# A two-block transformer on one core: SBUF addresses aligned to 2048 bytes, the first stages reordered, two norms taken together

## The chip, the cores and the metric

The kernel runs on one core of a Trainium2 chip, as one program launched once. The metric is its device time in microseconds (us). 302 weight tiles of 512 KB are streamed from HBM while the program runs.

## What is computed

512 tokens, width 1024, float32. A first block of two layers, then a second block of one layer:

```python
for i in range(2):                       # first block
    hn = rmsnorm(x, attn_norm_g[i])
    mix, q_cross = mla_mixer(...) if i == 0 else swa_mixer(...)   # 12 heads; full causal, or window 128 with alibi and sinks
    cross = memory_cross_attention(q_cross, rmsnorm(mem), w_mem_kv[i])   # 4 heads, 256 memory tokens
    x = x + concat(mix, cross) @ w_o[i]
    x = x + relu(rmsnorm(x, g) @ w_up) ** 2 @ w_down              # 4096 hidden
x = rmsnorm(x, final_norm_g)
h = rmsnorm(x, norm1_g)                  # second block: the norm of a norm
...                                      # gated convolution, compressed and windowed attention (8 heads), merge
x = x + mix @ w_o
x = x + (silu(conv(h2 @ w_g)) * (h2 @ w_u)) @ w_ffn_out           # 2816 hidden
```

In the first layer the queries come from a rank-384 and keys and values from a rank-256 projection, each with its own norm (`c_q`, `c_kv`); 32 of the 96 query and key features are rotated by position, and the rotated key part is the same for all heads.

## The kernel before

**Data.** Activations lie feature-major: 128 features on the partitions, 512 tokens along the row, `X[:, k, :]` for the k-th 128 features. Every matrix product is made of three in a reduced float32 format: an operand is split in a high part (rounded) and a low part (the rest), and `product` issues high x high, high x low, low x high (L526, L527, L528). `XH`/`XL` hold the split activation (8 slices), `HH`/`HL` the hidden layer of the two MLPs, `H2H`/`H2L` that of the last, `MIXH`/`MIXL` and `YAH`/`YAL`/`YBH`/`YBL` the merge of the second block.

**Weights.** A ring of four slots. SyncE loads tile n into `RAW` once the low part of tile n-4 is made; ScalarE copies it to `WH` (high part, L835); GpSimd (POOL) computes `WL = RAW - WH` in four pieces (L487). ScalarE calls `keep_ahead(o)` between its other operations: it makes high parts up to three tiles ahead of the tile that output o ends with, and waits there until the old tile of the slot has been used.

**Products.** `dense` walks through a stage's outputs in order. An output is 8 steps over k of three products each, 512 columns wide, into one of four PSUM banks; output o waits until output o-4 has been drained by VectorE (`drained`). Between outputs a stage can have steps in `after`: `sums(norm)` adds squares over the partitions, `scales(norm)` spreads the norm's factor over them, `rotate_query(h)` turns one head's query. The order of each engine's queue is written out by hand; engines wait for one another by counting semaphores alone.

**Norms.** The norm's factor per token is not applied to the operand but to the result. For each slice ScalarE squares into `SQ` (L870), VectorE adds into `ACC` (L1175, L1178), and the square waits for the add before. Then `sums`, VectorE's variance (L1192), ScalarE's root, VectorE's diagonal of factors (L1201), `scales`, and a copy to `RBC` (L1209). `x_hi` (L877) and `x_lo` (L1214) write XH and XL from X times the gain.

**Start.** `in0` (8 outputs: two for c_kv, three for c_q, the rotated key, two for the memory queries), `mem` (8 outputs of 256 columns: memory keys and values for both layers), `up0` (26 outputs: six of keys, four and four of values, twelve query heads), then the first attention. VectorE drains nearly all of it; its queue in order: `c_kv` scaling, `c_q` squares, memory drains (`mem_out`, L1241, L1432), splits of the memory queries (L1248) and of layer 0's memory keys (L1257), the angles for the rotation (16 operations, L1266 to L1275), key rotation, splits of layer 1's memory keys, key drains (L1227), value drains (L1472, L1475), the query operand (L1418, L1423), then head by head the query rotation (L1480 to L1490). ScalarE copies the rotated key rows to each of the 12 heads (L1029).

**Output projections** (`output_projection`, stages wo0, wo1). The next MLP reads XH/XL too, which hold the projection's operand. ScalarE waits until the last output's last product and then rewrites slices 0 to 3, VectorE follows, and then 4 to 7.

**Second attention** (64 units of up to 256 keys, four steps in a row over VectorE, ScalarE and TensorE each). Ahead of it VectorE drains eight outputs and splits each (L1243, L1248, L1249), six for the 12 heads (Q1), two for the memory queries (`QX`, used from unit 48 on), and then zeroes one column in three banks (L1535); TensorE waits for all of it.

**Between the blocks.** mlp1's last outputs are followed by the squares of `final`. `in2` (25 outputs) runs on; behind outputs 0 and 1 come sums and scales of `final`, behind 2 and 3 those of `norm1`, whose squares are made in between, serially. Then VectorE multiplies and sums the position embeddings of the compression (L1555, L1556), copies `RBC`, drains outputs 0 to 3 to R32 (L1583), multiplies X by the final norm (L1715), and makes the angles of the second block.

## Time and profile before

| | |
|---|---|
| device time, median of three runs | 2014.95 us (2013.19 to 2016.40) |
| device time of the profiled execution | 2013.64 us |
| its span, first to last instruction | 2011.7 us |
| TensorE busy | 97% |
| mean granted TensorE clock | 0.987 of full speed |
| VectorE, ScalarE, GpSimd busy | 44%, 38%, 46% |

A row of the timeline gives start and length in us, engine, line, operation, what is written from what, and in brackets how long the engine was idle before and what ended it. PE is TensorE's matmul, DVE VectorE, ACT ScalarE, POOL GpSimd. Buffer numbers are left out of names, so R is R32 or any like it. Matmuls overlap in such rows; the distance between starts is what one costs.

### The profile page before, as it was taken

The numbers are of one execution on the slowest core, as the hardware profiler recorded it, in microseconds if no ns is written. First come the engines' busy times: TensorE is split into PE (matmuls) and PEld (weight loads), VectorE is DVE, ScalarE is ACT, GpSimd is POOL, SyncE is SP. The second block draws the span as 40 slices with busy tenths as digits, with TensorE's granted clock in tenths as the row PEclk, the third lists the DMA queues.
The fourth block names the chain that finished last, engine by engine and source line by source line (L and its number), as shares of the span: only waits on it lengthen the run. The fifth ranks groups of instructions, "written<-read, shape, count | busy, mean of one in ns | idle before, by whom it ended". The sixth has DMA issues, their size and how long they took to land.

```text
span 2011.7 us, 27171 instructions
## 1 busy us (share of the span) xinstructions
PE 1946.1 (97%) x9314; PEld 1588.4 (79%) x9314; DVE 887.5 (44%) x1848; ACT 771.3 (38%) x1379; POOL 931.5 (46%) x1236
## 2 busy tenths in 40 slices
PE   7889999999999989999999998999999999999999
PEld 5756878888888878788888875678988888888887
DVE  5787733222225576322222268686722245444200
ACT  4446833232223467432232333335832233222221
POOL 5541045555555651555555554342045546655553
PEclk9989999999999999999999998999999999999999
DMA  5220022322222310222323232121022223223332
GB/s 212 95 74 22 1 84 85 101 97 94 94 94 84 102 51 18 89 95 94 98 94 101 91 115 73 42 74 43 2 73 95 94 84 105 94 94 100 98 104 74
DMA packets 46686, 167.67 MB, mean 83 GB/s; under 512 B 5312, under 2 KB 5632, under 8 KB 46336
## 3 DMA queue, kind: packets, MB, share of 16 engines
q1 hardware_dynamic: 45216, 162.55, 24.7%
q10 hardware_dynamic: 1376, 3.84, 0.5%
q8 instruction: 62, 1.02, 0.2%
q14 instruction: 32, 0.26, 0.0%
HBM read 164.28 MB, written 2.10 MB: 83 GB/s over the span
## 4 chain that ended last, share of the span: by engine, by line
PE 57%; DVE 4%; issue 2%; ACT 1%; DVEq 0%; ACTq 0%
PE bank L526 17%; PE bank L528 17%; PE bank L527 17%; PE bank L626 2%; PE bank L599 1%; PE bank L612 1%; ACT PROB L896 1%; PE bank L768 1%; DVE ACC L1178 0%; PE bank L623 0%; PE bank L730 0%; ACT XH L902 0%; DVE KNL L1257 0%; ACT SQ L870 0%; PE bank L722 0%
## 5 line engine op out<-in xcount | busy, mean ns | idle before, releaser
L487 POOL TENSOR_TENSOR WL<-RAW,WH 128x256 fp32r<-128x256 f32 x1208 | 913.8, 787 | 1036.0 <-ACT WH L835 1035.9
L526 PE MATMUL bank<-XH,WH 128*128 128x512 f32 (+1 forms) x1480 | 592.3, 400 | 42.1 <-POOL WL L487 13.7
L527 PE MATMUL bank<-XL,WH 128*128 128x512 f32 (+1 forms) x1480 | 581.3, 393 | 0.0
L528 PE MATMUL bank<-XH,WL 128*128 128x512 f32 (+1 forms) x1480 | 581.0, 393 | 0.0
L835 ACT ACTIVATE WH<-RAW 128x1024 fp32r<-128x1024 f32 x302 | 317.0, 1051 | 348.0 <-PE bank L528 345.5
L526 PEld LDWEIGHTS bank<-XH,WH 128*128 128x128 f32 (+1 forms) x1480 | 279.6, 189 | 117.1 <-issue 28.0
L527 PEld LDWEIGHTS bank<-XL,WH 128*128 128x128 f32 (+1 forms) x1480 | 279.5, 189 | 62.5 <-issue 4.1
L528 PEld LDWEIGHTS bank<-XH,WL 128*128 128x128 f32 (+1 forms) x1480 | 279.3, 189 | 61.5
L528 PE MATMUL bank<-HH,WL 128*128 128x512 f32 x512 | 202.2, 395 | 0.0
L526 PE MATMUL bank<-HH,WH 128*128 128x512 f32 x512 | 202.2, 395 | 0.0
L527 PE MATMUL bank<-HL,WH 128*128 128x512 f32 x512 | 202.2, 395 | 0.0
L1339 DVE TENSOR_TENSOR AB<-TMP 128x512 f32<-128x512 f32 x64 | 44.3, 692 | 264.1 <-ACT TMP L933 264.1
L1356 DVE TENSOR_TENSOR DT<-bank,RB 128x512 f32<-128x512 f32 x64 | 44.3, 692 | 230.7 <-PE bank L528 230.7
L933 ACT ACTIVATE TMP<-bank 128x512 f32<-128x512 f32 x64 | 38.3, 599 | 222.9 <-PE bank L528 222.8
L527 PEld LDWEIGHTS bank<-HL,WH 128*128 128x128 f32 x512 | 96.1, 188 | 23.4
L528 PEld LDWEIGHTS bank<-HH,WL 128*128 128x128 f32 x512 | 96.1, 188 | 23.3
L526 PEld LDWEIGHTS bank<-HH,WH 128*128 128x128 f32 x512 | 96.1, 188 | 23.3
L870 ACT ACTIVATE SQ<-X 128x512 f32<-128x512 f32 x48 | 30.3, 631 | 148.8 <-DVE ACC L1178 107.4
L526 PE MATMUL bank<-H2H,WH 128*128 128x512 f32 x176 | 69.8, 396 | 0.0
L527 PE MATMUL bank<-H2L,WH 128*128 128x512 f32 x176 | 69.8, 396 | 0.0
L528 PE MATMUL bank<-H2H,WL 128*128 128x512 f32 x176 | 69.8, 396 | 0.0
L1152 ACT ACTIVATE TMP<-TMP,GV 128x512 f32<-128x512 f32 x22 | 16.0, 726 | 121.5 <-DVE TMP L1609 121.5
(334 smaller groups left out, 2577.5 us busy)
## 6 DMA issues: line engine op xcount, KB each, us to landing
RAW<-stream SPq DMA_DIRECT2D x302, 512.0 KB, 3.6
X<-x SPq DMA_DIRECT2D x4, 512.0 KB, 7.5
out<-X SPq DMA_DIRECT2D x8, 256.0 KB, 4.4
MEM<-mem ACTq DMA_DIRECT2D x1, 1024.0 KB, 10.9
W<-cmp_w ACTq DMA_DIRECT2D x1, 1024.0 KB, 6.1
CT<-consts ACTq DMA_DIRECT2D x1, 656.0 KB, 13.2
POSB<-pos_rows ACTq DMA_DIRECT2D x2, 256.0 KB, 5.1
HR<-pos_rows ACTq DMA_DIRECT2D x1, 256.0 KB, 2.7
```

What stands on the lines that cost most here:

```text
L487: ins = pool.tensor_tensor(WL[:, slot, c], RAW[:, slot, c], WH[:, slot, c].bitcast(F32), ALU.subtract)
L526: pe.matmul(dst, lhs[0], rhs[0], start=start, stop=False)
L527: pe.matmul(dst, lhs[0], rhs[1], start=False, stop=False)
L528: return pe.matmul(dst, lhs[1], rhs[0], start=False, stop=stop)
L599: ins = pe.matmul(BANK[SCORES[i % ns]][:, u.keys], q, k, start=n_pass == 0, stop=n_pass == len(u.passes) - 1)
L612: ins = pe.transpose(BANK[TURNED[j % nt]][:, blk(kb)], row[:, blk(kb)], IDENT)
L626: ins = pe.matmul(BANK[HEAD_OUT[u.head % 2]][:, u.out_cols], u.values[kb], pt[j % len(pt)][:, blk(kb)], start=u.start and kb == 0, stop=u. ...
L835: act.activation(WH[:, slot, :], RAW[:, slot, :], ACT.Copy).then_inc(hi_done, 1)
L870: act.activation(SQ[:, 0:tokens], src, ACT.Square, scale=scale).then_inc(squared, 1)
L933: act.activation(TMP[:, m % 2, :], BANK[(o0 + m) % RING][:], ACT.Relu).then_inc(signal(name + "_relu"), 1)
L1339: dve.tensor_tensor(AB[:, m % 2, :], TMP[:, m % 2, :], TMP[:, m % 2, :], ALU.mult).then_inc(drained, 1)
L1356: dve.tensor_tensor(DT[:, m % 2, :], BANK[(o0 + 8 + m) % RING][:], RB2[:], ALU.mult).then_inc(drained, 1)
```

## The change

- **Addresses.** Every SBUF tensor whose row is a multiple of 2048 bytes starts at a multiple of 2048; the others at one of 32, as all did. CT, GV and GF are declared behind ACC, SQ, TMP, RBC and COS/SIN, some tensors move, and one is added (`KMV`).
- **Start.** MEM, the positions and the late constants are loaded through SyncE's queue behind the first weight tiles instead of ScalarE's. The first output is computed in three passes over k (all high x high, then high x low, then low x high). The squares of in0 and mem alternate between two buffers. The angles are made in two parts: one ahead of the drain of output 3, one ahead of the c_kv adds; ScalarE's two sines follow the c_q root and stand ahead of the query splits. `rotate_key`, `sums("c_q")` and `scales("c_q")` move to other outputs. ScalarE drains the values; one DMA places the key rows in the 12 heads. The splits of layer 0's memory keys go behind the query operand, those of layer 1 behind the first attention.
- **Output projections.** Each k-step of the last output signals that its slice of XH/XL has been read; ScalarE and VectorE rewrite slices 0 to 6 as these come, and slice 7 once X is final. `x_hi` and `x_lo` come before the square and the add, there and in the MLPs.
- **Second attention.** The two memory queries are drained to buffers of their own (`QX1`) and split inside the attention, ScalarE's part at units 3 and 6, VectorE's at 6 and 9; TensorE waits for them at unit 48.
- **Norms.** norm1's squares are made with those of final behind mlp1's last outputs, in separate buffers; both sums follow output 0 of in2, both scales output 1. The embeddings of the compression move behind output 3, the second block's angles ahead of mlp1's last chunk, the multiplication of X by the final norm into the merge.

```diff
-            return stack.enter_context(nc.sbuf_tensor(name, shape, dt))
+
+            row = 4 * math.prod(shape[1:])
+            return stack.enter_context(nc.sbuf_tensor(name, shape, dt, align_bytes=32 if row % 2048 else 2048))
...
+        QX1 = [KMV[:].rearrange("p a n -> p (a n)"), POSF1]
...
-            for j in range(1, RING):
-                load(j, j, stream[j])
+            load(1, 1, stream[1])
+            load(2, 2, stream[2])
+            sp.dma_start(MEM[:], mem).then_inc(mem_in, 16)
+            load(3, 3, stream[3])
+            sp.dma_start(POSB0[:], pos_rows[0]).then_inc(signal("pos_in"), 16)
+            sp.dma_start(POSI[:], pos_cols).then_inc(signal("pos_in"), 16)
+            sp.dma_start(CT[:, CONST_LATE:], consts[:, CONST_LATE:]).then_inc(signal("late_consts_in"), 16)
...
+            def first_output(steps):
+
+                pe.wait_ge(hi_done, 1)
+                for n_pass, (w, a) in enumerate(((WH, XH), (WH, XL), (WL, XH))):
+                    if n_pass == 2:
+                        pe.wait_ge(lo_done, 1)
+                    for t, c, width, k, o, _, _, _ in steps:
+                        if n_pass < 2:
+                            pe.wait_ge(signal("in0_x_hi" if n_pass == 0 else "in0_x_lo"), k + 1)
+                        ins = pe.matmul(BANK[o % RING][:], w[:, t % RING, c:c + width], a[:, k, :],
+                                        start=n_pass == 0 and k == 0, stop=n_pass == 2 and k == KD - 1)
+                ins.then_inc(products_done, 1)
+
             pe.wait_ge(consts_in, 32)
-            dense(lambda _: plan.steps["in0"], 0, operand(XH, XL),
...
-                  after={0: [scales("c_kv")], 2: [sums("c_q")], 4: [scales("c_q")], 6: [rotate_key]})
+                  after={0: [scales("c_kv")], 1: [rotate_key], 3: [sums("c_q")], 6: [scales("c_q")]})
...
                     if m == KD - 1 and not own_operand:
-                        act.wait_ge(products_done, plan.out_mark[o0 + KD - 1])
-                        for j in range(KD // 2):
+                        for j in range(KD - 1):
+                            act.wait_ge(signal(stage + "_operand_read"), j + 1)
                             x_hi(x_stage, norm, j)
                     act.wait_ge(drained, o0 + m + 1)
+                    if own_operand or m == KD - 1:
+                        x_hi(x_stage, norm, m)
                     square(norm, m, X[:, m, :])
-                    if own_operand:
-                        x_hi(x_stage, norm, m)
-                if not own_operand:
-                    for m in range(KD // 2, KD):
-                        x_hi(x_stage, norm, m)
...
+                            x_hi(stage_after, gain_after, m)
                             square(norm_after, m, X[:, m, :])
-                            if stage_after:
...
-            for h in range(NH):
-                act.activation(KT0[HD:QK, h, :], KR[HD:QK, :], ACT.Copy).then_inc(signal("key_placed"), 1)
-                keep_ahead(up0 + 3 + h // 2)
-                if h == 3:
+            act.dma_start(KT0[HD:QK, :, :], KR[HD:QK, :].unsqueeze(1).to_broadcast([ROPE, NH, S])
+                          ).then_inc(signal("key_placed"), 16)
+            for o in range(6, 14):
+                keep_ahead(up0 + o)
+                if o == 10:
                     c_hi(KKV, KQ)
-            for o in range(9, 14):
-                keep_ahead(up0 + o)
...
+            dve.wait_ge(signal("pos_in"), 32)
+            angles0(0)
...
+            angles0(1)
             add_square("c_kv", 0)
             add_square("c_kv", 1)
...
             mem_out(1)
             mem_out(2)
+            mem_out(3)
             scale_columns("c_q", P * KQ, factor=-MLA_SCALE)
-            mem_out(3)
             for j in range(2):
                 split_lo_q(j, PROB1[:, j, :], QX[:, 2 * j:2 * j + 2, :])
-            for j in range(2):
-                split_lo_k(2 + j, PROB1[:, 2 + j, 0:NMEM], KMH[:, 0, 2 * j:2 * j + 2, :], KML[:, 0, 2 * j:2 * j + 2, :])
-            dve.wait_ge(signal("pos_in"), 32)
-            angles(POSB0[:], POSF0[:], const("inv_mla"), ANG0[:, 0, :], ANG0[:, 1, :], COS0[:], SIN0[:], "angles0")
             for o in range(4, 6):
...
-                split_lo_k(4 + j, PROB1[:, j, 0:NMEM], KMH[:, 1, 2 * j:2 * j + 2, :], KML[:, 1, 2 * j:2 * j + 2, :])
+            mem_out(6)
+            scale_rows("c_q", ACC)
+            mem_out(7)
             up0 = plan.out0["up0"]
             for m in range(6):
                 both_halves(up0 + m, KT0[0:HD, :, :], m)
-            for b in range(NT):
-                dve.tensor_copy(V0[:, b, S:NH * HD], output(up0 + 6 + b)[:, 0:NH * HD - S]).then_inc(drained, 1)
             c_scale("c_q", KKV)
-            for b in range(NT):
-                dve.tensor_copy(V0[:, b, 0:S], output(up0 + 10 + b)[:]).then_inc(drained, 1)
-            dve.wait_ge(signal("key_placed"), NH)
+            for j in range(2):
+                split_lo_k(2 + j, PROB1[:, 2, j * NMEM:(j + 1) * NMEM], KMH[:, 0, 2 * j:2 * j + 2, :],
+                           KML[:, 0, 2 * j:2 * j + 2, :])
+            dve.wait_ge(signal("key_placed"), 16)
+            dve.wait_ge(drained, up0 + 14)
             for h in range(NH + 1):
...
             attention("mla")
+            for j in range(2):
+                split_lo_k(4 + j, KMV[:, j, :], KMH[:, 1, 2 * j:2 * j + 2, :], KML[:, 1, 2 * j:2 * j + 2, :])
             output_projection("wo0", "mlp0", "mlp0")
...
-                    split_value(in1 + 6 + m, s1 + 2 + m, PROB1[:, (2 + m) % 4, :], RBC, -SCALE)
-                if m >= 1:
-                    dst = Q1[:, 2 * m - 2:2 * m, :] if m <= 6 else QX[:, 2 * m - 14:2 * m - 12, :]
-                    split_lo_q(s1 + 1 + m, PROB1[:, (1 + m) % 4, :], dst)
+            for m in range(8):
+                split_value(in1 + 6 + m, s1 + 2 + m, PROB1[:, (2 + m) % 4, :] if m < 6 else QX1[m - 6], RBC, -SCALE)
+                if 1 <= m < 7:
+                    split_lo_q(s1 + 1 + m, PROB1[:, (1 + m) % 4, :], Q1[:, 2 * m - 2:2 * m, :])
             dve.wait_ge(drained, in1 + 14)
             for b in SCORES:
                 dve.memset(BANK[b][:, 2 * P:2 * P + 1], 0.0).then_inc(signal("column_zeroed"), 1)
...
+            def memory_queries(j):
+                return lambda: split_lo_q(s1 + 8 + j, QX1[j], QX[:, 2 * j:2 * j + 2, :])
+
+            attention("swa", {6: memory_queries(0), 9: memory_queries(1)})
...
             scale_columns("final", D, diagonal=TMP[:, 0, :])
-            for m in range(KD):
-                add_square("norm1", m)
-            scale_rows("final", TMP[:, 1, :])
-            scale_columns("norm1", D, of_normed=True)
-            dve.wait_ge(signal("w_cmp_in"), 32)
-            for x_, name in enumerate(("pe_k", "pe_v")):
...
-            own.step(dve.memset(VC[:], 0.0))
-            own.step(dve.memset(KCH[:].bitcast(F32), 0.0))
-            own.step(dve.memset(KCL[:].bitcast(F32), 0.0))
-            own.step(dve.tensor_scalar(gain("q"), gain("q"), -SCALE, None, ALU.mult))
+            scale_columns("norm1", D, of_normed=True, bank=7)
+            scale_rows("final", FINAL)
+            scale_rows("norm1", RBC, bank=6)
+
...
                 if what == "out" and j == 3:
-                    for m in range(KD):
-                        dve.scalar_tensor_tensor(X[:, m, :], X[:, m, :], gain("final", m), TMP[:, 1, :],
-                                                 ALU.mult, ALU.mult).then_inc(signal("x_normed"), 1)
-                    dve.wait_ge(signal("pos2_in"), 16)
-                    angles(POSB2, POSF2, const("inv_nsa"), PROB2[:, 0, :], PROB2[:, 1, :], COS2[:], SIN2[:],
-                           "angles2")
+                    prepare_compression()
...
+                dve.scalar_tensor_tensor(X[:, m, :], X[:, m, :], gain("final", m), FINAL[:], ALU.mult, ALU.mult
+                                         ).then_inc(signal("x_normed"), 1)
+            dve.wait_ge(signal("x_normed"), KD)
```

## Rows read from the trace of the kernel before

**Rows 1.** The page's busy times

```profile
PE 1946.1 (97%) x9314; PEld 1588.4 (79%) x9314; DVE 887.5 (44%) x1848; ACT 771.3 (38%) x1379; POOL 931.5 (46%) x1236
```

**Rows 2.** Waits of TensorE over the whole span: us, times, longest

```profile
PE bank L526 <- POOL WL L487: 13.7, 2, 13.3
PE bank L526 <- DVE PROB L1241: 8.6, 1, 8.6
PE bank L526 <- DVE R L1583: 8.3, 1, 8.3
PE bank L526 <- DVE KT L1227: 5.9, 2, 5.6
PE bank L599 <- DVE bank L1535: 4.6, 1, 4.6
PE bank L526 <- issue: 4.2, 2, 2.1
```

**Rows 3.** Windows over dense stages: length, PE busy (products), granted clock, DMA

```profile
389.53:433.06 43.53, 43.53 (x193) 1.00 0.30 96
433.06:477.86 44.80, 44.80 (x194) 1.00 0.29 95
1598.55:1643.53 44.98, 44.98 (x193) 1.00 0.28 94
1884.71:2008.40 123.69, 123.69 (x529) 1.00 0.28 92
```

**Rows 4.** Windows behind long gaps, TensorE alone

```profile
93.80:130.10 36.30, 21.44 (x85) 0.76 0.20 71
298.00:301.40 3.40, 3.40 (x9) 0.51 0.24 98
```

**Rows 5.** Timelines of ScalarE, GpSimd and TensorE at the start: start, us, what

```profile
13.54 1.33 ACT L877 ACTIVATE XH<-X,GV 128x512 fp32r<-128x512 f32 x2 [1.59 <-DMA X<-x]
...
16.69 1.04 ACT L835 ACTIVATE WH<-RAW 128x1024 fp32r<-128x1024 f32 x1
...
17.81 7.41 POOL L487 TENSOR_TENSOR WL<-RAW,WH 128x256 fp32r<-128x256 f32 x8 [4.67 <-ACT WH L835]
...
21.58 0.50 PE L526 MATMUL bank<-XH,WH 128*128 128x512 f32 x1 [0.38 <-POOL WL L487]
```

**Rows 6.** Timeline of VectorE ahead of the first attention

```profile
47.44 0.42 DVE L1209 COPY ACC<-bank 128x256 f32<-128x256 f32 x1 [3.31 <-PE bank L580]
...
86.59 6.55 DVE L1257 TENSOR_TENSOR KML<-PROB,KMH 64x256 fp32r<-64x256 f32 x8
93.17 0.43 DVE L1266 CAST POSF<-POSB 128x512 f32<-128x512 int32 x1
...
101.62 0.43 DVE L1275 TENSOR_SCALAR SIN<-SIN 128x512 f32<-128x512 f32 x1
...
108.20 6.84 DVE L1257 TENSOR_TENSOR KML<-PROB,KMH 64x256 fp32r<-64x256 f32 x8
...
123.70 1.47 DVE L1472 COPY V<-bank 128x256 f32<-128x256 f32 x4
...
128.05 1.47 DVE L1423 TENSOR_TENSOR XL<-TMP,XH 128x512 fp32r<-128x512 f32 x2
```

**Rows 7.** Second attention: VectorE's timeline; window (PE, PEld, DVE, ACT, POOL)

```profile
724.02 1.43 DVE L1248 TENSOR_TENSOR QX<-PROB,QX 64x512 fp32r<-64x512 f32 x1
...
732.00:745.00 13.00, 12.49 (x104) 11.67 (x105) 12.90 (x65) 11.95 (x46) 4.99 (x8) 1.00 0.00 1
```

**Rows 8.** Timeline of VectorE between the two norms and R32

```profile
1212.36 0.69 DVE L1178 TENSOR_TENSOR ACC<-ACC,SQ 128x512 f32<-128x512 f32 x1 [0.79 <-ACT SQ L870]
...
1219.65 1.76 DVE L1555 TENSOR_TENSOR PROB<-W,GV 128x1024 f32<-128x1024 f32 x1
```

**Rows 9.** Two products in a row in a down stage, TensorE's timeline

```profile
450.32 0.40 PE L528 MATMUL bank<-HH,WL 128*128 128x512 f32 x1
450.56 0.39 PE L526 MATMUL bank<-HH,WH 128*128 128x512 f32 x1
```

More of the change, by code:

```diff
@@ L17 @@
+import math
 from contextlib import ExitStack
@@ L179, with square_no, squares_end @@
 NORM_K = dict(NORMS)
+def square_no(norm, m):
+    if norm in ("final", "norm1"):
+        return SQUARES0["final"] + 2 * m + (norm == "norm1")
+    return SQUARES0[norm] + m
+def squares_end(norm):
+    return SQUARES0["norm1"] + KD if norm == "final" else SQUARES0[norm] + NORM_K[norm]
 def over(fn, i, n=NCH):
@@ L452, in program, with squares_of, squares_sum @@
             IN2 += AFTER_OUT.get(o, [])
+        def squares_of(norm, m):
+            if norm == "norm1":
+                return TMP[:, 0, :]
+            return TMP[:, 1, :] if norm in ("in0", "mem") and m % 2 else SQ
+        def squares_sum(norm):
+            return TMP[:, 1, :] if norm == "norm1" else ACC
         block = ctx.enter_context(nc.Block())
@@ L528, in product, with dense @@
                 return pe.matmul(dst, lhs[1], rhs[0], start=False, stop=stop)
-            def dense(steps_of, i, act, n_tok=S, token_major=(), ready=None, after=None, seen=None):
+            def dense(steps_of, i, act, n_tok=S, token_major=(), ready=None, after=None, seen=None, o0=None, released=None):
                 seen = set() if seen is None else seen
@@ L577, in step @@
                     if n:
-                        pe.wait_ge(scale_used, n)
+                        pe.wait_ge(scale_used, n - (norm == "norm1"))
                     pe.wait_ge(diag_done, n + 1)
-                    pe.matmul(BANK[5][:, 0:tokens], ONES, diagonal[:, 0:tokens], start=True, stop=True
+                    pe.matmul(BANK[bank][:, 0:tokens], ONES, diagonal[:, 0:tokens], start=True, stop=True
                               ).then_inc(scale_done, 1)
@@ L689, in _ @@
             rotate_query(NH - 1)()
-            attention("mla", (drained, plan.out0["wo0"]), (signal("split_lo"), SPLIT_AT["in1"]))
-            dense(lambda _: plan.steps["wo0"], 0, operand(XH, XL), ready=heads_ready("mla"))
+            attention("mla", (drained, plan.out0["wo0"]), (signal("split_lo"), SPLIT_AT["mem"] + 2))
+            dense(lambda _: plan.steps["wo0"], 0, operand(XH, XL), ready=heads_ready("mla"),
+                  released=signal("wo0_operand_read"))
             mlp("mlp0")
@@ L698, in _ @@
             attention("swa", (drained, plan.out0["wo1"]), (signal("column_zeroed"), len(SCORES)),
-                      (signal("split_lo"), SPLIT_AT["in2"]))
-            dense(lambda _: plan.steps["wo1"], 0, operand(XH, XL), ready=heads_ready("swa"))
+                      (signal("split_lo"), SPLIT_AT["in2"] - 2))
+            dense(lambda _: plan.steps["wo1"], 0, operand(XH, XL), ready=heads_ready("swa"),
+                  released=signal("wo1_operand_read"))
             mlp("mlp1")
@@ L748, in compress @@
                               start=True, stop=True).then_inc(signal("cmp_sums"), 1)
-            after = {0: [sums("final")], 1: [scales("final", diagonal=TMP[:, 0, :])],
-                     2: [sums("norm1")], 3: [scales("norm1")]}
+            after = {0: [sums("final"), sums("norm1", bank=7)],
+                     1: [scales("final", diagonal=TMP[:, 0, :]), scales("norm1", bank=6)]}
             def turn_gates(_):
@@ L1051, in _ @@
             std("in1")
-            for o in range(15):
-                if o < 14:
-                    keep_ahead(in1 + o)
+            for o in range(14):
+                keep_ahead(in1 + o)
                 if 1 <= o < 3:
@@ L1072, in _ @@
             std("final")
-            for m in range(KD):
-                square("norm1", m, X[:, m, :], scale=gain("final", m))
-            keep_ahead(in2 + 2)
             std("norm1")
@@ L1186, in scale_columns @@
                 if of_normed:
-                    own.then(dve.tensor_scalar(VAR[:, 0:nt], BANK[4][:, 0:nt], 1.0 / width, None, ALU.mult))
+                    own.then(dve.tensor_scalar(VAR[:, 0:nt], BANK[bank][:, 0:nt], 1.0 / width, None, ALU.mult))
                     for _ in range(2):
@@ L1261, in split_lo_k, with angles @@
                 ins.then_inc(signal("split_lo"), 1)
[L1263 removed]
+            def angles(pos, posf, inv, angle, turns, cos, sin, done, parts=(0, 1)):
                 c1 = TWO_PI_PARTS
[L1266 to L1268 removed]
+                if 0 in parts:
+                    own.then(dve.tensor_copy(posf, pos))
+                    own.then(dve.tensor_scalar(angle, posf, inv, None, ALU.mult))
+                for dst, quarter in [((cos, 0.25), (sin, 0.0))[part] for part in parts]:
                     own.then(dve.tensor_scalar(turns, angle, 1.0 / (2 * np.pi), quarter, ALU.mult, ALU.add))
@@ L1312, in output_projection @@
                 for m in range(KD + 1):
+                    if m == KD - 1 and not own_operand:
+                        for j in range(KD - 1):
+                            x_lo(x_stage, norm, j)
                     if m < KD:
```

205 lines of the change are left out of this document (108 added, 97 removed).

## Prediction

> **What bounds the kernel now.** I read the page's busy times first: TensorE is busy 1946.1 of 2011.7 us [rows 1], so a microsecond counts only if it shortens TensorE's own sequence. That sequence can shorten in three ways: idle time goes, a product takes less time, or less work runs at the halved clock. The waits of TensorE give the first [rows 2]: some 48 us, of which 13.7 is mostly the start, 8.6 a wait for a VectorE copy in the memory projection, 8.3 a wait for R32, 5.9 for the key copies, 4.6 for the zeroed column ahead of the second attention, 4.2 twice 2.1 behind an output projection. The windows over whole dense stages give the second [rows 3]. A stage is 192 products of 512 columns (528 in the last), plus at most two that overlap an edge. An "up" stage, operand XH/XL, takes 43.53/192 = 0.2267 us a product. The "down" stage beside it, operand HH/HL, takes 44.80/192 = 0.2333, the stage on MIXH/MIXL 44.98/192 = 0.2343, the last, on H2H/H2L, 123.69/528 = 0.2343. All are 100% busy at full clock, so this is no wait. The third: after a long gap the clock is at its lower level for a while (0.51 over 3.4 us behind the output projection, 0.76 on average in 93.8 to 130.1, which holds two gaps and half-clock stretches) [rows 4].
>
> **Alignment.** What separates the fast operand from the slow ones? Not the work beside it: the last stage has almost none and is slow. From the declared sizes (rounded to 32 bytes), XH, XL, WH and WL all sit at one offset modulo 2048 bytes. HH sits 1408 further on (CT 6368 + GV 896 + GF 32 + SM 224 + POSI 32 = 7552), H2H at 1440, MIXH at 928. The change puts all of them at a multiple of 2048, so each has the relation to WH that XH has today. I charge them XH's rate: HH/HL 1536 products x 6.6 ns = 10.2; H2 528 x 7.6 = 4.0; MIX 192 x 7.6 = 1.4; YA and YB 192 x about 6.6 = 1.3 (not shown apart; by HH's rate). Sum **16.9 us**. The bounds are 0 (the offset is not the cause) and 16.9 + 29.3 (XH's 4440 products would gain another 6.6 ns each).
> A rule speaks against this term: the Trainium skill, page "SBUF — State Buffer", section "SBUF: two separate sides", says contention is structural and that PE's ports wait on nobody. All these offsets are multiples of its 16-byte line, so by it the term is 0. The trace disagrees in that equal products differ by 6.6 ns, but it cannot show that the address is why. That is the second rival.
>
> **From the start to the first attention.** Today TensorE waits for the low half of tile 0, since each of output 0's products by k needs it, and starts its second output at 21.58, when POOL has finished tile 1: high half at 16.69, POOL from 17.81 [rows 5]. Ahead of that high half ScalarE lost 1.59 us waiting for the last of x, with which 1 MB of MEM shared the DMA engines, and some more for an add. With both gone the high half is at about 14.3, POOL's 3.7 us end at 19.1, and TensorE, which has meanwhile done output 0 pass by pass, goes on about 2.3 earlier; two short waits behind it (the sum of squares, C32) go too. Head start at output 4, an estimate: 3.2.
> Then VectorE's queue decides [rows 6]. The angles are 16 operations, 93.17 to 102.05, 8.9 us. Their first part (4.9) moves ahead of c_out(3), where VectorE idles 3.31 today. The second (4.0) stands ahead of the c_kv squares, and TensorE's sums("c_kv") waits for those. My step-by-step times: the adds end near 63.5, TensorE arrives at 60.4, **a new wait of 3.1**; and the c_kv diagonal comes 1 us later than today, for three drains now follow the adds. The head start is gone; TensorE begins memory output 4 about 1.2 later than today.
> Behind it the gain comes. VectorE is busy without a break from 82.84 to 129.5, and its XL for the queries ends this queue [rows 6]. Out of it go the key splits of layer 0 (6.55) and layer 1 (6.84), the angles (8.9) and V copies (1.47): 23.7. Against that: 1.2 late, 2.7 waiting for ScalarE (its sines now stand ahead of the query split: 1.3 table load, two of 0.6), about 1.5 for ScalarE's V copies between the c_hi steps. XL is ready near 110. TensorE itself needs, from 93.0: six outputs of 1.36, four of 0.72, four of 1.36, 16.5 us, and arrives at 109.8. Output 14 starts at 109.8 instead of 130.2; 1.2 us of waiting for ScalarE's TMP goes as well: 21.7. The key splits of layer 0 (6.6) now stand ahead of the query rotation and make VectorE 4 us late there; it catches up 0.8 a head, and bank and rotation are needed four heads later: nothing. The key rows become one DMA of 0.8 MB, nearly 20 us ahead of its use: nothing. POOL takes about 3.7 us a tile [rows 5] and each tile of this stretch arrives 1 to 3 us early: nothing, with little cover. A gap of 3 us or the thin outputs at 100 to 104 may lower the clock once more (3.4 us at half, 1.7). I take **20**, with 12 and 23 as bounds.
>
> **Output projections.** XH's slices are now rewritten as the last output releases each, so ScalarE's 0.7 and VectorE's 0.8 run under its 5.45 us. The slice of k = 7 comes 2.4 to 4 us after its last product and is needed 4.8 after. Both 2.1 us waits (2.25 between products) go [rows 2], and at the first the stretch at clock 0.51 (3.4 us, so 1.7) [rows 4]: 4.0 + 2.2. The order "XL before the add" takes about 0.7 from the wait at the second layer's start. **6.9**. The moved key splits of layer 1 (6.8 VectorE, 3.4 ScalarE) lie under the first four outputs of wo0, 21.8 us.
>
> **Second attention.** Four QX operations, 3.6 us, come out from between the last value and the zeroed columns [rows 7]. They return at units 6 and 9, with 2.5 us on ScalarE. There VectorE is busy 12.90 of 13 us and ScalarE 11.95 [rows 7]: nearly no cover. I take **1** (bounds -1 and 4).
>
> **Two norms together.** Today norm1's eight squares and eight adds alternate until 1213.05; the diagonal follows until 1219.7; two operations of 1.8 us for each of two position embeddings, 7.3 us, then stand ahead of RBC, and TensorE waits 8.3 us for R32, until 1229.25 [rows 8, 2]. After the change the squares lie under mlp1's last outputs: VectorE's share there is 0.7 + 0.9 + three of 0.7 to 1.2, about 5.2 of 5.45, just covered. TensorE waits 0.3 for the last add, takes both sums behind output 0 and both diagonals behind output 1 (a wait of 0 to 1.5), and runs outputs 2 and 3; RBC is there by 1210, so output 4 starts at 1219.9 at the latest 1221: 9.4. The half clock behind the old gap goes; by the stretch of [rows 4] I put 1.9. The embeddings now delay only R32[4], whose bank is needed 21 us later. The angles (9 to 12 us) move ahead of mlp1's last chunk, where four free banks (22.7 us) cover them. The rescaling of X (8 x 0.75) moves into merge, 16.5 us a step with 5 of VectorE. **11.5** (8 to 13). The 2 us waits in the rest of in2 come from work that stays.
>
> **Sum.** 16.9 + 20 + 6.9 + 1 + 11.5 = 56.3; the profiled execution took 2013.64, so 1957.3. The median of the runs shown is 1.3 higher: **1958 us**.
>
> **Rivals.**
> 1. *Queues give less*: the c_kv wait grows, the clock falls again, the attention takes all back. Bounds: 12 + 5 - 1 + 8 = 24 instead of 39.4: 1974. For it: VectorE's full queue; against it: TensorE's idle rows are large and plain.
> 2. *The address does nothing*: 1958 + 16.9 = 1975. For it: the trace changes address and tensor together (by the rule of the skill this is the outcome); against it: four operands, one rate per offset, whatever runs beside them.
> 3. *Both*: 1991.
> 4. *XH gains as well*, because its own offset was not a multiple of 2048: 1958 - 29 = 1929. Nothing in the trace shows a faster product at full clock.
> 5. *Slower*: multiples of 2048 are a bad offset for all products. Single products of the slow operands take 0.24 [rows 9]. If all 6888 did: 4440 x 13.3 + 2448 x 6.4 ns = 75 us, against 39.4 saved: 2049. It decides once the mean rises over today's 229.2 ns by 39.4/6888 = 5.7, beyond every stage mean shown. Against it: XH and WH share an offset today.
>
> **How the numbers follow.** Forecast (1946 to 1968) 0.58, rival 1 0.15, rival 2 0.12, rival 3 0.05, rival 4 0.07, rival 5 0.03. The range 1940 to 1980 holds the forecast and rivals 1 and 2. Faster by over 0.2% (what a measurement here tells from no change) needs 4 us: all but rival 5 and a little for what I have not seen: 0.94; same 0.02, slower 0.04.
>
> **What would show it.** HH, H2H and MIXH stages at 0.2267 a product; no wait at R32 or behind wo0/wo1; a new wait of about 3 us for the c_kv adds; first attention from 147 instead of 167; the second attention longer by 2 to 3 us. Wrong if those stages keep 0.233, or the XH stages change.

## The result, and the profile after

The changed kernel takes **1970.4 us** (median of 4 runs, 1969.3 to 1970.7) against 2015.7 (2013.2 to 2017.5) before: ratio 0.9775, 95% interval 0.9758 to 0.9792. Forecast was 1958, with 1940 to 1980 as range. 56.3 us were forecast, 43.2 are gone from the span (2011.7 to 1968.5).

Two measures are used below. Rows of waits give TensorE's idle time alone. A "gap" in the text is the time from the start of one product to the start of the next, so it is 0.3 to 0.6 us longer than the idle time in it.

The page's busy times (answers to [rows 1]), and the waits of TensorE ([rows 2]; the first row is the time until the first product):

```profile
PE 1932.1 (98%) x9314; PEld 1590.0 (81%) x9314; DVE 897.3 (46%) x1840; ACT 770.5 (39%) x1375; POOL 944.3 (48%) x1236
```

```profile
PE bank L703 <- ACT WH L884: 9.1, 1, 9.1
PE bank L559 <- DVE XL L1271: 4.4, 6, 1.3
PE bank L604 <- DVE ACC L1235: 3.5, 1, 3.5
PE bank L775 <- DVE TMP L1691: 3.0, 1, 3.0
PE bank L559 <- POOL WL L520: 1.2, 1, 1.2
PE bank L637 <- DVE POSB L1300: 1.0, 1, 1.0
```

The waits of 8.6, 8.3 and 5.9 us are gone. Of the 13.7 at the start, 9.1 until the first product and 1.2 for the next weight tile are left. The 4.6 ahead of the second attention are 1.0 now, the 2.1 behind each output projection 1.2. Two large waits are new or grown: 3.5 for the c_kv adds (forecast 3.1) and 3.0 in in2. Windows over dense stages, as in [rows 3]: HH, XH, MIXH, H2H; columns length, PE busy (products), granted clock, DMA share, GB/s.

```profile
325.63:369.15 43.52, 43.52 (x194) 1.00 0.30 97
369.15:412.67 43.52, 43.52 (x194) 1.00 0.30 97
1560.84:1604.36 43.52, 43.52 (x194) 1.00 0.30 97
1845.57:1965.02 119.45, 119.45 (x529) 1.00 0.29 95
```

All operands now run at XH's rate, 43.52/192 = 0.2267 us a product. The last stage ends with the program, so its window runs from the start of its first to the start of its last product, 527 distances: 119.45/527, the same. Windows of TensorE at the lower clock level (answers to [rows 4]):

```profile
63.20:70.00 6.80, 5.68 (x26) 0.50 0.41 140
285.10:288.50 3.40, 3.40 (x9) 0.50 0.12 13
704.90:711.70 6.80, 6.07 (x28) 0.50 0.00 0
1172.60:1176.00 3.40, 3.40 (x9) 0.50 0.76 280
1281.80:1292.00 10.20, 9.87 (x18) 0.50 0.12 45
```

Each lies behind or around a gap of TensorE: 3.9, 1.6, 0.8 and 1.2, 1.7, and 3.4 us. Two more stretches, 3.4 us from 152.0 and 10.2 from 1315.9, have their like before (171.6, 1352.6). In all, half clock went only from 51.5 us of the span to 45.1.

With both traces divided at the first product of each stage, the 43.2 us are (a dense layer is counted from its first HH stage on):

| from, to | before | after | saved | forecast |
|---|---|---|---|---|
| start, first attention | 167.12 | 148.26 | 18.9 | 20 |
| to the first HH stage (wo0) | 177.62 | 177.37 | 0.25 | 4.0 |
| HH of two dense layers, YA and YB, MIX, H2H | | | 16.9 | 16.9 |
| second layer's start, second attention | 136.94 | 136.79 | 0.15 | 1.7 |
| wo1 | 91.91 | 91.25 | 0.7 | 2.2 |
| in2 and third attention | 290.02 | 283.65 | 6.4 | 11.5 |

The third row is 5.13 + 5.13 + 1.16 + 1.46 + 4.01, in the order named. The forecast of 6.9 for the output projections is split over rows 2, 4 and 5.

### The profile page after: what moved, and what is told of

Its sections match the earlier page's. It is cut to its first block, busy times and chain, and to the rows that moved or that the text cites. A ratio compares the mean times of both kernels' runs of the same rounds, so it can differ in the third digit from the quotient of the medians.

```text
span 1968.5 us, 27142 instructions
## 1 busy us (share of the span) xinstructions
PE 1932.1 (98%) x9314; PEld 1590.0 (81%) x9314; DVE 897.3 (46%) x1840; ACT 770.5 (39%) x1375; POOL 944.3 (48%) x1236
## 4 chain that ended last, share of the span: by engine, by line
PE 90%; DVE 5%; issue 3%; ACT 2%; POOL 0%; DVEq 0%; POOLq 0%; ACTq 0%
PE bank L559 26%; PE bank L560 26%; PE bank L561 26%; PE bank L664 4%; PE bank L637 3%; PE bank L650 2%; DVE XL L1271 1%; ACT PROB L948 1%; PE bank L821 1%; PE bank L731 0%; PE bank L604 0%; POOL WL L520 0%; DVE KT L1284 0%; PE bank L616 0%; PE bank L661 0%
## 5 line engine op out<-in xcount | busy, mean ns | idle before, releaser
L520 POOL TENSOR_TENSOR WL<-RAW,WH 128x256 fp32r<-128x256 f32 x1208 | 927.0, 799 | 980.3 <-ACT WH L884 980.1
L559 PE MATMUL bank<-XH,WH 128*128 128x512 f32 (+2 forms) x1472 | 586.3, 398 | 5.7 <-DVE XL L1271 4.4
L560 PE MATMUL bank<-XL,WH 128*128 128x512 f32 (+2 forms) x1472 | 576.2, 391 | 0.0
L561 PE MATMUL bank<-XH,WL 128*128 128x512 f32 (+2 forms) x1472 | 575.8, 391 | 0.0
L559 PEld LDWEIGHTS bank<-XH,WH 128*128 128x128 f32 (+2 forms) x1472 | 276.5, 188 | 79.5 <-issue 10.4
L560 PEld LDWEIGHTS bank<-XL,WH 128*128 128x128 f32 (+2 forms) x1472 | 276.6, 188 | 61.7 <-issue 4.1
L561 PEld LDWEIGHTS bank<-XH,WL 128*128 128x128 f32 (+2 forms) x1472 | 276.6, 188 | 60.3
L560 PEld LDWEIGHTS bank<-HL,WH 128*128 128x128 f32 x512 | 96.1, 188 | 19.8
```

What stands on the lines that cost most here:

```text
L520: ins = pool.tensor_tensor(WL[:, slot, c], RAW[:, slot, c], WH[:, slot, c].bitcast(F32), ALU.subtract)
L559: pe.matmul(dst, lhs[0], rhs[0], start=start, stop=False)
L560: pe.matmul(dst, lhs[0], rhs[1], start=False, stop=False)
L561: return pe.matmul(dst, lhs[1], rhs[0], start=False, stop=stop)
```

## The experiments

All but e1 are edits of the changed kernel. Where no range of runs or interval is given, the kernel ran once.

### Alignment: e1 to e5

**e1**: the kernel before, with pads alone.

```
+        tensor(ctx, "PAD1", [P, 160])
         with ExitStack() as block1:
...
+                    tensor(merged, "PAD2", [P, 120])
                     MIXH = tensor(merged, "MIXH", [P, KD, S], F32R)
...
+            tensor(ffn, "PAD3", [P, 504])
             H2H = tensor(ffn, "H2H", [P, FF2, S], F32R)
```

> The kernel before with pads alone: 640 bytes ahead of the block tensors, 480 ahead of MIXH, 2016 ahead of H2H, so that HH, HL, YAH, YAL, YBH, YBL, MIXH, MIXL, H2H, H2L all start at 1152 modulo 2048, as XH, XL, WH and WL do; nothing starts at a multiple of 2048 and no instruction is moved. My theory (what counts is the distance between the streamed operand and the weights): HH, MIXH and H2H stages at 0.2267 us a product instead of 0.2333 to 0.2343, the time 16.9 below before, about 1999. Rival 2 of the prediction (the address does nothing): 2015.7, rates unchanged. A third reading (only multiples of 2048 help): 2015.7 too.

2002.7 us (4 runs, 1995.9 to 2003.1) against 2013.0 (ratio 0.9933, 0.9908 to 0.9957). Windows over XH, HH (first and second), MIXH and H2H:

```profile
388.38:431.90 43.52, 43.52 (x194) 1.00 0.29 97
431.90:475.42 43.52, 43.52 (x194) 1.00 0.31 97
1592.76:1636.28 43.52, 43.52 (x193) 1.00 0.29 97
1877.46:1996.91 119.45, 119.45 (x529) 1.00 0.29 95
```

The first two rows are an XH and an HH stage. Addresses alone give the full rate, and none of these operands starts at a multiple of 2048. But the median fell by 10.3, the span of the profile by 11.2, not 16.9. In the profile 16.9 is there stage by stage; 1.5 is given back up to the end of wo1, and 4.1 in in2, with more half clock (68.3 us in all, where before has 51.5; 17.1 in one stretch, where before has 10.2):

```profile
1342.30:1359.40 17.10, 17.10 (x68) 0.50 0.10 32
```

How much of this is chance isn't settled: the fourth run, 1995.9, is 17.1 under before's median, and the interval (8.7 to 18.5 us saved) holds 16.9.

**e2**: the rule taken out of the changed kernel.

```
-            return stack.enter_context(nc.sbuf_tensor(name, shape, dt, align_bytes=32 if row % 2048 else 2048))
+            return stack.enter_context(nc.sbuf_tensor(name, shape, dt, align_bytes=32))
```

> The changed kernel with its alignment rule alone taken out (every tensor at the next 32 bytes), its queues and its order of tensors kept. HH then starts 1408 bytes behind XH and WH modulo 2048, as in the kernel before. My theory: HH, MIXH and H2H stages back at 0.2333 to 0.2343, XH stages stay at 0.2267, the time about 1970.4 + 16.9 = 1987. Rival 2 (the address does nothing, the rates fell for another reason): 1970.

1985.6 us (ratio 0.9857, 0.984 to 0.9873), 15.2 more than with the rule. An XH stage, the HH stage behind it, and the MIXH stage:

```profile
911.77:955.31 43.54, 43.54 (x194) 1.00 0.29 97
955.31:1000.10 44.79, 44.79 (x194) 1.00 0.30 95
1575.01:1619.81 44.80, 44.80 (x194) 1.00 0.27 94
```

Rival 2 is out: the address is the cause. The MIXH stage takes 44.80 and not the 44.98 of before: by the declared sizes, the changed order of tensors has moved MIXH from 928 to 1408 bytes behind the weights.

**e3, e4**: the rule stays, but for HH, MIXH and H2H and their low parts it is replaced by pads that put them the stated number of bytes behind a multiple of 2048, and so that far from the weights.

> The changed kernel with HH and HL moved 1024 bytes away from a multiple of 2048, MIXH and MIXL 256, H2H and H2L 64; XH, WH and WL stay at multiples of 2048. Reading A (any distance but 0 modulo 2048 is slow): all three stages at 0.233 to 0.234 a product, the time 1970 + 5.1 x 2 + 1.5 + 4.1 = 1986. Reading B (the weight tiles start at every multiple of 512, so only the distance modulo 512 can count): HH stays at 0.2267, MIXH and H2H slow: 1976. Reading C (slow only from a distance that is no multiple of some small line of 64 or 128 bytes): HH and MIXH fast, 1970 to 1975.

> The same with HH and HL 32 bytes away, MIXH and MIXL 128, H2H and H2L 512. Reading A: all three slow, 1986. Reading B: H2H fast at 0.2267, HH and MIXH slow: 1982. Reading C: H2H and MIXH fast, HH slow: 1981.

1972.8 and 1984.7 us. e3, HH at 1024, MIXH at 256, H2H at 64:

```profile
859.43:902.95 43.52, 43.52 (x193) 1.00 0.30 97
1561.98:1605.51 43.53, 43.53 (x194) 1.00 0.30 97
1846.71:1967.35 120.64, 120.64 (x528) 1.00 0.29 94
```

e4, HH at 32, MIXH at 128, H2H at 512:

```profile
953.63:998.43 44.80, 44.80 (x193) 1.00 0.30 95
1573.81:1618.60 44.79, 44.79 (x194) 1.00 0.29 94
1859.82:1979.27 119.45, 119.45 (x528) 1.00 0.29 95
```

1024, 512 and 256 are fast, 128 and 32 slow at 0.2333, 64 between, 120.64/527 = 0.2289. None of the three readings holds: A is wrong (1024 is fast), B is wrong (256 is fast), C is wrong (128 is slow). What fits is the distance to the weights modulo 256. It also orders the rows of before: HH was 1408, so 128, from the weights (0.2333), H2H 1440 and MIXH 928, both 160 (0.2343); and MIXH in e2, at 128, went to 0.2333. Distances of 96, 192 and 224 were not tried.

**e5**: the weights moved. Own address or distance?

```
         (the rule taken out as in e2)
+        tensor(ctx, "PADW", [P, 32])
         WH = tensor(ctx, "WH", [P, RING, TW], F32R)
...
+        tensor(ctx, "PAD1", [P, 160])
         with ExitStack() as block1:
```

> The changed kernel without its alignment rule, with pads so that WH and WL start at 1280 modulo 2048, XH and XL at 1152 as in the kernel before, HH, HL, YAH, YAL, YBH, YBL, MIXH and MIXL at 1280, H2H and H2L at 1312. So XH keeps its own address and is 128 bytes from the weights; HH is level with them. My theory, as the runs with shifted operands left it (fast at a distance from the weights that is a multiple of 256 bytes, slow at 32, 64, 128, 160): the XH stages fall to 0.233 a product, HH and MIXH are at 0.2267, H2H at 0.2343: 1970 + 4440 x 6.5 ns + 4 = 2003. Rival (an operand's own address decides, not its distance to the weights): XH stays at 0.2267, the time is about 1975.

1996.5 us. Windows over XH, HH, MIXH, H2H:

```profile
909.85:954.64 44.79, 44.79 (x194) 1.00 0.28 94
954.64:998.17 43.53, 43.53 (x193) 1.00 0.29 97
1577.44:1620.96 43.52, 43.52 (x194) 1.00 0.30 97
1868.13:1991.09 122.96, 122.96 (x528) 1.00 0.27 92
```

XH has the address that it had before, 1152, and became slow; HH, level with the weights, is fast; H2H, 32 bytes away, has 122.96/527 = 0.2333, where 0.2343 was expected. So it is the distance of the streamed operand to the weights. The total is 6.5 under the sum that was expected. Some 3 of that lie ahead of the first attention, which began at 147.65, no later than with fast products (148.26), where the sum counts 2.2 for 336 products. That part waits for other engines, and 108 of these products, the query heads' with 96 columns of weights, did not become slower: 0.231 to 0.232 with either address. The rest is spread over the stages and was not traced.

### Queues: e6 to e12

**e6**: the order in the output projection. The edit in short, not word for word:

```
 VectorE:  for j in range(4): x_lo(x_stage, norm, j)        # was range(KD - 1)
           X[:, 7, :] += bank                               # as before
+          for j in range(4, KD): x_lo(x_stage, norm, j)
           add_square(norm, m - 1)
 ScalarE: +x_hi of 0 and 1, then keep_ahead(o0 + 7), then x_hi of 2 to 6
```

> The changed kernel; in wo0 and wo1 VectorE adds the last output to X after four of the seven XL slices instead of after all seven, and makes XL of k = 7 before the square's add; ScalarE makes XH of k = 0 and 1 ahead of its weight copy instead of behind it. My theory (the 1.5 us gap of TensorE at k = 7 of the next stage is VectorE's queue: seven XL at 0.75 to 1.23 us stand ahead of the add): both gaps of 1.5 us fall below 0.5 and the half clock of 3.4 us behind the first goes, 3 to 5 us less than 1970.4, about 1966. Rival (the total of VectorE's work from the first released slice sets the end, so the order moves nothing): 1970.

1968.1 us (1964.7 to 1969.9; ratio 0.9758, 0.9742 to 0.9775). From the first attention's end to the first HH stage 92.60 instead of 92.78, behind wo1 91.21 instead of 91.25: nothing. (The profile's span, 1968.0, differs from 1968.5 by parts that the edit leaves alone: the start took 2.2 longer and in2 with the third attention 2.5 less.) The wait was divided, between the operand and the sums of the norm (waits of TensorE, 270 to 300):

```profile
PE bank L604 <- DVE ACC L1239: 0.9, 1, 0.9
PE bank L559 <- DVE XL L1275: 0.5, 1, 0.5
```

The rival is right: order alone moves nothing here. In the changed kernel VectorE's timeline reads as follows, with GpSimd's below:

```profile
274.87 6.18 DVE L1271 SCALAR_TENSOR_TENSOR XL<-X,GV,XH 128x512 fp32r<-128x512 f32 x7 [2.32 <-ACT XH L927]
280.97 0.67 DVE L1378 TENSOR_TENSOR X<-X,bank 128x512 f32<-128x512 f32 x1
281.57 0.68 DVE L1235 TENSOR_TENSOR ACC<-ACC,SQ 128x512 f32<-128x512 f32 x1
282.50 0.75 DVE L1271 SCALAR_TENSOR_TENSOR XL<-X,GV,XH 128x512 fp32r<-128x512 f32 x1 [0.26 <-ACT XH L927]
```

```profile
274.30 4.22 POOL L520 TENSOR_TENSOR WL<-RAW,WH 128x256 fp32r<-128x256 f32 x4 [2.61 <-ACT WH L884]
```

The last product of wo0 ends near 276.6. The add of its output waits until 280.97, behind seven XL, of which the three that lie wholly beside GpSimd's tile take 1.2 us each instead of 0.75. XL of k = 7 is done at 283.25; the product ahead of the one that needs it began at 281.75.

**e7**: the second half of the angles behind the c_kv column scales, no longer ahead of the c_kv adds.

```
-            angles0(1)
             add_square("c_kv", 0)
...
             scale_columns("c_kv", P * KKV)
+            angles0(1)
             mem_out(0)
```

> The changed kernel with the second half of the angles of layer 0 (4 us of VectorE) behind the c_kv column scales instead of ahead of the c_kv adds. My theory (these 4 us make TensorE's gap of 3.9 us at the c_kv sums and the 6.8 us at half clock behind it): no gap over 1 us and no half clock at 60 to 70; but VectorE's queue up to XL of the queries is as long as before, so only a part reaches the first attention: it starts 1 to 4 us earlier than 148.3. Time 1966 to 1969. Rival (the whole 3.9 + 3.4 is gained): 1963. Rival (VectorE's queue sets the start of output 14 alone): 1970.

1966.9 us (1964.3 to 1969.1; ratio 0.9757, 0.9741 to 0.9773). VectorE's last c_kv add, which ended at 64.3 in the changed kernel, and the angles, now behind it:

```profile
58.97 1.14 DVE L1235 TENSOR_TENSOR ACC<-ACC,SQ 128x512 f32<-128x512 f32 x1 [0.70 <-ACT SQ L920]
...
65.56 0.96 DVE L1327 TENSOR_SCALAR ANG<-ANG 128x512 f32<-128x512 f32 x1
```

The gap of 3.9 and the half clock at 63 to 70 are gone; two gaps, 1.7 (c_kv scales) and 2.3 (c_q sums), came instead. The first attention starts at 145.7 instead of 148.3: the expected part. But six kernels whose start is the changed kernel's (e3, e4, e6, e8, e9, e10) began it between 147.3 and 150.5, and e12, which has e7's edit, at 147.3, with 6.8 us of half clock behind the same two gaps. So the edit's worth is not clear of chance.

**e8**: the convolution of two channel tiles behind the rotation and norm of the next head, on VectorE. The edit in short, not word for word:

```
-                        UP = PROB2[0] * PROB2[1]; convolve(PROB2[0], UP, ...)      # in out(10), out(13)
+                        pending.append((o, m))          # done behind "rotate" 1 and "spread" 4
```

> The changed kernel; in in2 VectorE's product and convolution of two channel tiles (4.3 us) run behind the rotation and norm of the head that stand behind them today. My theory (TensorE's gap of 3.4 us at 1278.8 waits for that queue, and the 10.2 us at half clock follow from the gap): gap and half clock go, 3.4 + 5.1 = 8.5 at most; the splits of the last heads end at VectorE's pace, so 4 to 8 are left: 1962 to 1966. Rival (VectorE is the bound over the whole stretch to the compressed scores): 1969 to 1970.

1970.4 us (1967.7 to 1971.2; ratio 0.9773, 0.9757 to 0.979). The gap of 3.4 at 1278.8 is gone, but gaps of 3.0 (1261.3) and 2.0 (1289.3) stand instead of 2.3 and none. From the start of in2 to the compressed scores it takes 147.8 us against 149.3 in the changed kernel, but that doesn't judge it: e6 and e7, which leave in2 as it is, show 146.9. There the same code has gaps of 2.3 and 1.5 with 6.8 us at half clock, where the changed kernel's profile has 2.3 and 3.4 with 10.2. Up to the MIXH stage the same code took 397.9 (changed kernel), 397.1 (e7) and 395.4 (e6); e8 took 398.0. Whether e8 is worth anything stays open.

**e9**: the memory queries of the second attention split ahead of it again.

> The changed kernel with the memory queries of the second attention split ahead of it, as in the kernel before (their two raw halves stay in their new buffers). My theory (moving them only moves 3.6 us of VectorE from the front of the attention into it, where VectorE is full): the gap ahead of the attention is back at about 5 us, the attention at 63.6 us instead of 67.2, the time within 1 us of 1970.4. Rival (the lengthening of the attention has another cause): the gap comes back and the attention stays at 67, about 1974.

1970.9 us (1970.0 to 1972.9; ratio 0.9779, 0.9763 to 0.9795). Gap and attention both went back: the gap is 4.95 us where the changed kernel has 1.4. Windows of the whole attention, of the changed kernel and then of e9:

```profile
699.85:767.06 67.21, 62.55 (x477) 57.07 (x477) 61.17 (x275) 59.95 (x211) 15.31 (x22) 0.95 0.02 8
```

```profile
702.85:766.62 63.77, 60.96 (x477) 56.55 (x477) 58.20 (x271) 57.47 (x207) 14.42 (x20) 0.96 0.01 2
```

So the change had saved 3.6 us of gap and lost 3.4 us of attention.

**e10**: norm1's squares, adds, sums and scales behind those of final as in the kernel before; the position embeddings stay where the change put them. The edit in short:

```
-            after = {0: [sums("final"), sums("norm1", bank=7)],
-                     1: [scales("final", ...), scales("norm1", bank=6)]}
+            after = {0: [sums("final")], 1: [scales("final", ...)], 2: [sums("norm1")], 3: [scales("norm1")]}
```

> The changed kernel with norm1's squares and adds behind those of final, its sums behind output 2 and its scales behind output 3, as in the kernel before; the position embeddings stay behind output 3, out of the way. My theory by now (the 8.3 us wait at output 4 came from the embeddings standing ahead of RBC, and taking the norms together costs VectorE the cover under the last outputs: gaps of 1.7 and 0.8 and 3.4 us at half clock): outputs 0 to 4 of in2 take at most 1.5 us more than the 28.9 of the changed kernel, and the time is within 2 us of 1970.4. Rival, as the prediction put it (the norms taken together are what saves): the wait at output 4 comes back in part, 3 to 7 us, 1974 to 1977.

1970.4 us (1970.0 to 1970.9; ratio 0.9774, 0.9758 to 0.979). From output 0 of in2 to the start of output 4: windows of the changed kernel and of e10.

```profile
1162.95:1191.80 28.85, 27.10 (x116) 0.94 0.38 129
```

```profile
1162.90:1192.68 29.78, 26.30 (x118) 1.00 0.34 125
```

Apart costs 0.9 us here and nothing in the total; before, with the norms apart too, the stretch took 36.1. What differs is what stands between the norm's diagonal and the copy to RBC. In e10 it is 1.3 us of waiting for TensorE; before, it is the four operations of the position embeddings, 7.4 us [rows 8]:

```profile
1187.11 2.82 DVE L1255 TENSOR_SCALAR ACC<-CT,SM 128x128 f32<-128x128 f32 x4
1191.21 0.69 DVE L1263 COPY RBC<-bank 128x512 f32<-128x512 f32 x1 [1.28 <-PE bank L612]
```

**e11**: the two key splits of layer 0 back ahead of the scaling for the queries.

> The changed kernel with VectorE's key splits of the memory of layer 0 (6.6 us) back ahead of the scaling of the queries' operand. My theory (VectorE's queue up to XL of the queries sets when output 14 of up0 starts, and this is where the largest term comes from): TensorE gets a new wait of about 5 to 6 us ahead of output 14, the clock falls behind it, and the first attention starts 5 to 8 us later than at 148.3; the time 1975 to 1979. Rival (ScalarE's value copies set it): 1970 to 1972.

1974.6 us. The first attention starts at 153.04, 4.8 later; 1.9 of that came from the start (the second weight tile was later), 2.9 from here, less than expected. The new wait, and VectorE:

```profile
PE bank L559 <- ACT V L1092: 3.0, 1, 3.0
```

```profile
108.14 4.00 DVE L1314 TENSOR_TENSOR KML<-PROB,KMH 64x256 fp32r<-64x256 f32 x8
112.17 2.27 DVE L1485 SCALAR_TENSOR_TENSOR TMP<-C,GV,ACC 128x512 f32<-128x512 f32 x2
```

The wait ends with ScalarE's copy of a value output, which frees output 14's bank. But that copy stands behind ScalarE's XH of the queries, and this waits for VectorE's TMP, behind the eight splits: theory and rival are one chain. Two things made it cheap. The eight took 4.00 us where [rows 6] has 6.55: in e11 seven took 0.42 us each with GpSimd idle and the last 0.85 beside its next tile; before, seven took 0.85 beside a tile and the last 0.42 behind it. And there was slack: in the changed kernel VectorE waits 1.96 us for ScalarE's XH at 109.6, and TensorE has no wait to speak of at output 14 (0.07 us).

**e12**: e6 and e7, and the norm's sums of the dense layers one output later.

```
-                chunk(0, set(), {0: [sums(name)], 1: [scales(name)]})
+                chunk(0, set(), {1: [sums(name)], 2: [scales(name)]})
```

> The changed kernel with the two edits of e6 and e7 together, and with the norm's column sums in the two dense layers one output later (behind output 1, the scales behind output 2), since in e6 the gap of 1.5 us only moved from the operand to these sums, which wait for the last square's add. My theory: the gaps behind wo0 and wo1 shrink to the 0.9 us of e6 and none stands at the sums; 2 x 1.3 us less than e6's form, and e7's 2.6: about 1964, at best 1961 if the half clock behind wo0 goes too. Rival (VectorE and ScalarE work up their delay elsewhere, and the waits come back in the next stage): no better than e7, 1967.

**1964.0 us** (5 runs, 1960.3 to 1966.1; ratio 0.9747, 0.9732 to 0.9762), under the changed kernel's 1970.4 (1969.3 to 1970.7); the intervals of the two ratios just overlap. The half clock behind wo0 is gone (behind wo1 the changed kernel had none), and one gap of 0.9, at XL of k = 7, is left at each:

```profile
278.00:292.00 14.00, 13.48 (x63) 1.00 0.24 76
809.20:823.00 13.80, 13.27 (x62) 1.00 0.32 96
```

From attention to HH stage 89.86 and 89.84 instead of 92.78 and 91.25: 2.9 and 1.4. The start gave 0.9 in this profile, not e7's 2.6.

## Why the prediction was right, and where it was not

**As a whole.** The time is inside the range, but above the 1946 to 1968 that had 0.58 of the chances. The addresses gave their 16.9; the queues gave 26.3 where 39.4 was forecast, nearer to the 24 of rival 1, "queues give less", than to the forecast.

**Alignment, 16.9.** Right in size and stage by stage; e1 and e2 show that the address does it. The relation was named too narrowly: I took the offset modulo 2048, and e3 and e4 show modulo 256. The Trainium skill, page "SBUF — State Buffer", section "SBUF: two separate sides", has that PE's ports never wait on anyone, and from this the prediction read 0; the measurement decides against 0 for this case: the same product costs 0.2267, 0.2289, 0.2333 or 0.2343 by address alone. What in the chip does it, no run shows. What of the 16.9 reaches the total is less sure: 11.2 in the profile of e1, 15.2 between the medians of e2 and the changed kernel, and in both cases the runs don't exclude 16.9.

**Start to first attention, 20.** 18.9. The new wait came as forecast (3.5 for 3.1). The clock fell around it for 6.8 us, where the working allowed 3.4. Output 14 began at 112.8 instead of 109.8 (the working's own terms, 93.0 and 16.5, make 109.5), and not for want of XL: TensorE waits 0.07 us there. It came late itself, since up0 began at 94.66 instead of 93.0 and the four thin outputs took 4.3 us instead of 2.9, with two short waits in them. The six kernels with the same start would give 16.6 to 19.8 for this term. Of the parts of the change only two were undone (e7, e11); what each of the others is worth is not shown.

**Output projections, 6.9.** Wrong by 6.0: 0.9 came, and none of the 2.2 for waits and 1.7 for the clock at wo0. The step that failed: "The slice of k = 7 comes 2.4 to 4 us after its last product and is needed 4.8 after". It came 6.6 after. Seven XL stand ahead of the add in VectorE's queue, first released late by a weight copy on ScalarE, and slowed by GpSimd's tile. By the same section of the Trainium skill ("SBUF — State Buffer", "SBUF: two separate sides"), an instruction of VectorE with two inputs from SBUF and one of GpSimd that reads SBUF block each other. The trace agrees that each slows the other: 14 XL of the changed kernel ran with GpSimd idle, at 0.74 to 0.75 us, and the 32 that it covered for over half their time have a median of 1.22; the three pieces of GpSimd's tile beside XL at 275 to 278 took 1.2 us each, the first, nearly free of it, 0.74. e6 and e12 show what was missing: order alone moves the wait, and only with the sums moved too does most of it go.

**Second attention, 1.** 0.15 from the second layer's start on, and e9 shows why: 3.6 out of the gap, 3.4 into the attention. Against the kernel before it is 3.6 longer (63.63 to 67.21), where 2 to 3 was expected.

**Two norms, 11.5.** 6.4 came, below the range of 8 to 13. The gain at output 4 is 36.1 - 28.85 = 7.3 where I had 9.4 + 1.9 = 11.3: "just covered" failed on the same slowed VectorE work (XL and square adds 1.2 us instead of 0.7, beside GpSimd's tile):

```profile
1164.49 1.23 DVE L1271 SCALAR_TENSOR_TENSOR XL<-X,GF,XH 128x512 fp32r<-128x512 f32 x1
1165.64 1.22 DVE L1235 TENSOR_TENSOR ACC<-ACC,SQ 128x512 f32<-128x512 f32 x1
1169.07 0.68 DVE L1235 TENSOR_TENSOR ACC<-ACC,SQ 128x512 f32<-128x512 f32 x1
1169.20 0.50 PE L559 MATMUL bank<-XH,WH 128*128 128x512 f32 x1 [1.32 <-DVE XL L1271]
```

So there was a gap of 1.7 at k = 7 and one of 0.8 at the sums, and the clock fell again. e10 corrects the cause: the saving isn't in taking the norms together; what is left to explain it is the position embeddings, which left the way of RBC (putting them back alone was not tried). Another 0.9 went in the rest of in2, less than the 2.5 by which kernels with the same code there differ.

The sum held since the two large terms did; no term's error hid another's. The missing 13.1 us are 6.0 + 5.1 + 1.1 + 0.9: the first two are mostly new waits in the place of the ones removed, with the clock falling behind them, the last is work that only moved.

## What to carry to other kernels

List the start addresses of what TensorE streams beside those of its weights: a distance of a multiple of 256 bytes was worth 3% of each 512-column fp32r product here, for a pad. A removed wait counts only up to the next engine's result: cost that engine's whole queue up to it, with durations taken beside the work that will run there, and ask last what a gap of 1.5 us does to the clock. Where several things are changed at once, undo each: here the addresses and VectorE's work moved out of the way paid, while the later memory queries (e9) and the norms taken together (e10) were worth nothing that the total shows.

## What the runs showed of the hardware that was not expected

- Products of 512 columns at full clock, by the distance between streamed operand and weights modulo 256 bytes: 0 (distances 0, 256, 512 and 1024): 0.2267 us; 32 and 128: 0.2333; 64: 0.2289; 160: 0.2343 [rows 3; e1 to e5].
- Half-clock stretches came as 3.4, 6.8, 10.2, 13.7 and 17.1 us, and gaps of about the same size had different ones behind them: 3.9 us had 6.8 (changed kernel) or 3.4 (e8) behind it, and gaps of 1.7 and 2.3 us had none (e7) or 6.8 (e12), each pair at the same place in the same code. That leaves some 2 us of chance in a profile, as large as several of the effects sought here.
- VectorE's operations with two SBUF inputs and GpSimd's split slow each other: XL of 128x512 takes 0.75 us alone and 1.22 beside GpSimd, a split of 64x256 0.42 and 0.85, so the same eight took 4.00 us or 6.55 by what GpSimd did meanwhile [rows 6; e11]. In the changed kernel at 275 to 278, an XL and a piece of GpSimd's tile both came about every 1.16 us, where each alone comes every 0.66 to 0.70: slower than alone, but sooner than one after the other.
